# Low rows of features and gated values at a byte distance of their own from the weights

## The chip, the cores and the metric

The kernel runs on one NeuronCore of a Trainium2 chip. The metric is the device time of one execution in microseconds (us). Three executions of the kernel before took 1446.21, 1448.00 and 1448.74 us, median 1448.0.

## The reference

Two transformer blocks in float32 work on 256 context tokens and 256 latent tokens of width 1024. The first block mixes by a two-directional mLSTM and window attention, with a gated feed-forward network of width 2816. The second block has two layers, a retention and SSD mixer and multi-head latent attention, each with a SwiGLU network. Cut to the shape of the work that concerns us:

```python
def conv_glu(h, w_up, conv_w, conv_b, w_down):
    a, val = jnp.split(h @ w_up, 2, axis=-1)
    a = jax.nn.gelu(dwconv(a, conv_w, conv_b))
    return (a * val) @ w_down

def swiglu(h, w_gate, w_up, w_down):
    return (jax.nn.silu(h @ w_gate) * (h @ w_up)) @ w_down

x = x + g_a * (jnp.concatenate([y_m, y_a], axis=-1) @ w_out)
x = x + g_f * conv_glu(modulate(rmsnorm(x, norm_ffn), sh_f, sc_f), w_up, ffn_conv_w, ffn_conv_b, w_down)
...
u = modulate(rmsnorm(x, norm_mix), sh_a, sc_a) @ w_in
```

Nearly all of the arithmetic is such products of 1024 or 2816 features with weights.

## The kernel before

Activations stand transposed: 128 features on the partitions, 512 tokens (256 context, then 256 latent) along them. Every float32 operand of a linear product is split into a high part, rounded to the format that TensorE reads in one pass (fp32r), and a low part, the rest. A product is then three matmuls that add up in one PSUM bank: high weights with high features, high weights with low features, low weights with high features. I call such three matmuls over one tile of 128 features a k step. A unit of weights (128 outputs by 1024 features) has 8 k steps; `down` takes 22 tiles of gated values in parts of 8, 7 and 7.

The linear phases follow each other in a fixed order (`weight_phases`). Block 0 (latent tokens, 256 columns, except `ka` and `km`, which take all 512): `va_gates`, `ka`, `qa`, `vma`, `km`, `vmb`, `qm`, `om`, `out0`, `up0`, `down0`. Block 1 (512 columns): `in1`, `vra`, `vrb`, `out1`, `up1`, `down1`. Block 2: `ckv` (512), `cq`, `uk`, `uv`, `uq`, `out2`, `up2`, `down2` (256). In `out2`, `up2` and `down2` the high weights meet the high and the low features in one matmul instruction of two halves of 256 columns (`two_halves`, lines 621 to 624); the product that completes a tile of the output in `down2` is made of three. Other phases put high and low products of a unit in turn (`high_then_low`, lines 762 and 763) and then the 8 products of the low weights (768). In `va_gates`, `vma`, `vmb`, `vra` and `vrb` (`token_linear`) the roles are exchanged: features are loaded into the array and weights are streamed.

Weights go through three slots of 4096 bytes in each of `raw`, `w_hi` and `w_lo`. SyncE loads a unit into `raw` when GpSimd has split the unit that held the slot; ScalarE rounds it to `w_hi` (line 1502); GpSimd subtracts to get `w_lo` in two halves of 512 columns (line 2050); TensorE takes it. The order is written out, nothing is scheduled dynamically.

The features' high and low rows are two arrays of 8 x 512 floats in one room, `h_both`, the low array directly behind the high one (`rows_from`). The gated values are two arrays of 22 x 512 in `hidden_both` (`hidden`). Where the arrays start is set for each phase by constants: `MIXING` for the mixing phases of the three blocks, `UP_AT`, `DOWN_AT` and `OUT_AT` for the others. In a phase of 256 latent columns the latter three move the columns: they start at float 240 of each row in place of 256 (`columns`).

In bytes within a partition, the build places `w_hi` at 13440, `w_lo` at 25728, `hidden_both` at 87680 and `h_both` at 177792. A weight tile stands at a multiple of 512 from its slot, a feature row at a multiple of 2048. So the distance from the streamed row to the weights loaded for the next product, taken modulo 256, is one number for a phase. I call this the distance (loaded address minus streamed address, modulo 256).

Of the kernel before, what the change touches and what calls it, by code (L numbers as in the profile page):

```python
# [15 lines left out]
KD = D // P  # L16
CTX = LAT = 256
TOK = CTX + LAT
# [5 lines left out]
KF = FF // P  # L24
# [74 lines left out]

H_ROOM = 16
HIDDEN_ROOM = 0
MIXING = (16, 0, 16)
UP_AT = (240, 0, 240)
DOWN_AT = (240, 0, 240)
OUT_AT = (240, 0, 240)


CARRIED = {"ka": (1, 2), "qa": (2, 1), "vma": (1, 2), "km": (1, 3), "vmb": (1, 2), "qm": (1, 1), "om": (1, 1),  # L110
# [88 lines left out]
def build(nc, dram, small_at, tables_at, layers=3):  # L199
# [4 lines left out]
    with ExitStack() as stack:  # L204
# [3 lines left out]
        def sbr(name, shape):  # L208

            return stack.enter_context(nc.sbuf_tensor(name, shape, F32R))  # L210
# [31 lines left out]
        with nc.sbuf_tensor("arena", [P, ARENA], F32) as arena:  # L242
            pass
        with nc.sbuf_tensor("hidden_both", [P, HIDDEN_ROOM + 2 * KF * TOK], F32R) as hidden_room:
            pass

        def hidden(n):

            a = DOWN_AT[1] if n == 1 else 0
            both = hidden_room[:, a:a + 2 * KF * TOK].rearrange("p (a k t) -> p a k t", a=2, k=KF)  # L250
            return both, both[:, 0], both[:, 1]

        stack.enter_context(nc.sbuf_tensor("arena_end", [P, HIDDEN_ROOM + ARENA], F32))

        with nc.sbuf_tensor("scratch", [P, H_ROOM + 2 * KD * TOK], F32) as scratch_room:
            scratch = scratch_room[:, OUT_AT[1]:OUT_AT[1] + 2 * KD * TOK]
        h_room = sbr("h_both", [P, H_ROOM + 2 * KD * TOK])

        def rows_from(a):
            both = h_room[:, a:a + 2 * KD * TOK].rearrange("p (a k t) -> p a k t", a=2, k=KD)  # L260
            return both, both[:, 0], both[:, 1]

        def features(name):

            if name[:-1] in ("up", "out"):
                at = (UP_AT if name[:-1] == "up" else OUT_AT)[int(name[-1])]
                return rows_from(at if name in ("up1", "out1") else 0)
            return rows_from(MIXING[1 if name in ("in1", "vra", "vrb") else 2 if name in ("ckv", "cq") else 0])

        
        with nc.sbuf_tensor("work_r", [P, 3, TOK], F32R) as work_r:
            pass
        work = sb("work", [P, 3, TOK])
# [104 lines left out]
        ckv, rope_s, kpe, kswap = c(2, TOK), c(4, LAT), c(TOK), c(LAT)  # L378
# [96 lines left out]
        def columns(name, t0, t1):  # L475

            at = {"u": UP_AT, "d": DOWN_AT, "o": OUT_AT}[name[0]][int(name[-1])]
            return slice(at, at + LAT) if t0 == L0 else slice(t0, t1)
# [115 lines left out]
        def _(pe):  # L594
# [110 lines left out]
            def first_linear(gate):  # L705
                _, h_hi, h_lo = features("va_gates")

                f = ph["va_gates"]
                chunks = {0: (8, 9, 10, 11), 2: (12, 13, 14, 15)}
                for k in range(KD):  # L710
                    for q in chunks.get(k, ()):
                        ada_chunk(q)
                    if k == 2:
                        ada_columns(1)
                    u, n = divmod(k, KD // 2)
                    if n == 0:
                        pe.wait_ge(s["split"], 2 * (f.first_unit + u + 1))
                    w_h, w_l = (part_slot(x, f, u)[:, n * 144:n * 144 + 256] for x in (w_hi, w_lo))
                    gate(k)
                    for i in range(TT):  # L720
                        last = three(bank[i // 2][:, i % 2 * 256:i % 2 * 256 + 256], h_hi[:, k, i * P:(i + 1) * P],
                                     h_lo[:, k, i * P:(i + 1) * P], w_h, w_l, k == 0 and i % 2 == 0,
                                     k == KD - 1 and i % 2 == 1)
                        if k == KD - 1 and i % 2:
                            last.then_inc(s["steps"], 1)
# [21 lines left out]
            def linear(name, t0, t1, K=KD, both=None, hi=None, lo=None, M=P, gate=None, after=None, first=0, early=False):  # L747


                f = ph[name]  # L750
                both = features(name)[0] if both is None else both
                hi, lo = (both[:, 0], both[:, 1]) if hi is None else (hi, lo)
                n, parts = t1 - t0, f.parts
# [84 lines left out]
            def token_linear(name, K=KD, hi=None, lo=None, gate=None, after=None):  # L838

                f = ph[name]  # L840
                hi, lo = features(name)[1:] if hi is None else (hi, lo)
                pair = 2 if f.steps == 2 else 1
                for u in range(0, f.units, pair):
                    pe.wait_ge(s["split"], 2 * (f.first_unit + u + pair))
                    if pair == 2:
                        a, b = ((f.first_unit + u + i) % SLOTS for i in range(2))
                        two = slice(a, b + 1) if b > a else slice(a, None, -a)
                        w_h, w_l = ([x[:, two, 0:f.width].rearrange("p s (k n) -> p k s n", k=K)[:, k]
                                     for k in range(K)] for x in (w_hi, w_lo))
                    else:  # L850
                        w_h, w_l = ([part_slot(x, f, u, K)[:, k] for k in range(K)] for x in (w_hi, w_lo))
                    cols = pair * f.width // K
                    for i in range(TT):
                        t = f.first_taken + u * f.takes + i
                        room(t)
                        out = bank_of(t)[:, 0:cols]
                        if pair == 2:
                            out = out.rearrange("p (s n) -> p s n", s=2)
                        for k in range(K):
                            if gate and u == 0 and i == 0:  # L860
                                gate(k)
                            last = three(out, hi[:, k, i * P:(i + 1) * P], lo[:, k, i * P:(i + 1) * P],
                                         w_h[k], w_l[k], k == 0, k == K - 1)
                        last.then_inc(s["steps"], 1)
                    if after:
                        after(u)
# [534 lines left out]
            def ffn(n, t0, t1):  # L1401
                feature_sums(t0, t1, f"up{n}")
                linear(f"up{n}", t0, t1, gate=next_h(), early=True)
                linear(f"down{n}", t0, t1, K=KF, both=hidden(n)[0],
                       gate=lambda k: pe.wait_ge(s["hid_done"], KF * n + k + 1))
# [80 lines left out]
        def _(act):  # L1486
# [97 lines left out]
            def round_hidden(n, i, t0, t1):  # L1584

                act.wait_ge(s["hid_in"], KF * n + i + 1)
                act.activation(hidden(n)[1][:, i, columns(f"down{n}", t0, t1)], work[:, i % 3, t0:t1], ACT.Copy).then_inc(s["hid_round"], 1)  # L1587
# [548 lines left out]
        def _(dve):  # L2136
# [601 lines left out]
            def hidden_low(n, i, t0, t1):  # L2738

                dve.wait_ge(s["hid_round"], KF * n + i + 1)  # L2740
                own = columns(f"down{n}", t0, t1)
                low(hidden(n)[2][:, i, own], work[:, i % 3, t0:t1], hidden(n)[1][:, i, own]).then_inc(s["hid_done"], 1)
# [565 lines left out]
```

## Time and profile before

| | |
|---|---|
| Three executions, median | 1448.0 us |
| The profiled execution | 1450.16 us |
| its span, first to last instruction | 1448.4 us |
| mean granted clock of TensorE | 0.996 |
| TensorE, GpSimd, VectorE, ScalarE busy | 97%, 58%, 59%, 45% |

The span is about 1.8 us shorter than the execution's time. The durations of matmul rows are modelled ends of pipelined instructions: 389 ns for 512 columns is not what a product costs. The distance between two starts is. A row that merges several products gives the start of the first, and the next row's start closes the stretch. The counts of a stretch include up to three products that begin before it.

### The profile page before, as it was taken

What the parts mean: (1) busy time and instruction counts of PE and PEld (TensorE: products, weight loads), DVE (VectorE), ACT (ScalarE), POOL (GpSimd) and SP (SyncE); (2) the same over time, 40 slices, a digit from 0 to 9 for tenths busy, and PEclk for the clock granted to TensorE, in tenths of its full rate; (3) what the DMA queues carried; (4) which work ended last, traced back from release to release, by engine and by line L of the source; (5) the groups of instructions that cost most, each with busy time, mean ns of one, the idle gap of its engine ahead of it and who ended that gap; (6) DMA issues with size and microseconds to landing.
All of it is one profiled execution on the core that took longest, in us unless ns stands there. A gap on an engine that the chain in (4) does not pass through costs nothing.

```text
span 1448.4 us, 21620 instructions
## 1 busy us (share of the span) xinstructions
PE 1400.3 (97%) x8272; PEld 1167.9 (81%) x8272; DVE 847.7 (59%) x1638; ACT 657.7 (45%) x1069; POOL 839.2 (58%) x672
## 2 busy tenths in 40 slices
PE   5999999999999999889999999999999999999998
PEld 3977798999988889446788888888888966888887
DVE  3788667776668888687665333321136677644422
ACT  3555755455552234783332322322226386555442
POOL 1534426999855444785355544544446620799996
PEclk9999999999999999999999999999999999999999
DMA  9748415777767753001355555533333320456664
GB/s 366 289 166 302 173 42 201 252 259 232 260 227 248 238 178 106 18 30 59 131 198 189 195 195 188 196 108 97 103 95 115 118 81 8 140 182 188 188 193 127
DMA packets 71207, 242.01 MB, mean 167 GB/s; under 512 B 7488, under 2 KB 12992, under 8 KB 70720
## 3 DMA queue, kind: packets, MB, share of 16 engines
q1 hardware_dynamic: 68688, 236.63, 48.8%
q10 hardware_dynamic: 2416, 4.00, 0.9%
q8 instruction: 66, 1.08, 0.3%
q14 instruction: 37, 0.30, 0.1%
HBM read 238.50 MB, written 1.05 MB: 165 GB/s over the span
## 4 chain that ended last, share of the span: by engine, by line
PE 51%; DVE 4%; ACT 1%; issue 1%; POOL 0%; DMA 0%; DVEq 0%; ACTq 0%
PE bank L762 9%; PE bank L768 9%; PE bank L763 9%; PE bank L623 8%; PE bank L624 4%; PE bank L614 2%; PE bank L616 1%; PE bank L615 1%; DVE h_both L2282 1%; PE cond_a L1160 1%; PE bank L622 1%; PE bank L1160 1%; PE bank L1168 1%; PE cond_a L1221 1%; PE bank L1180 1%; PE cond_b L1180 1%
## 5 line engine op out<-in xcount | busy, mean ns | idle before, releaser
L2050 POOL TENSOR_TENSOR w_lo<-raw,w_hi 128x512 fp32r<-128x512 f32 (+2 forms) x610 | 775.7, 1301 | 577.5 <-ACT w_hi L1502 567.7
L1502 ACT ACTIVATE w_hi<-raw 128x1024 fp32r<-128x1024 f32 (+3 forms) x300 | 307.7, 1029 | 590.8 <-PE bank L768 345.9
L762 PE MATMUL bank<-h_both,w_hi 128*128 128x512 f32 (+1 forms) x1000 | 321.9, 340 | 0.4 <-ACT w_hi L1502 0.4
L763 PE MATMUL bank<-h_both,w_hi 128*128 128x512 f32 (+1 forms) x1000 | 321.2, 339 | 0.0
L762 PEld LDWEIGHTS bank<-h_both,w_hi 128*128 128x128 f32 x1000 | 188.1, 188 | 22.1 <-ACT w_hi L1502 0.6
L763 PEld LDWEIGHTS bank<-h_both,w_hi 128*128 128x128 f32 x1000 | 188.3, 188 | 21.3
L768 PE MATMUL bank<-h_both,w_lo 128*128 128x512 f32 (+1 forms) x1000 | 197.7, 340 | 0.3 <-POOL w_lo L2050 0.3
L768 PEld LDWEIGHTS bank<-h_both,w_lo 128*128 128x128 f32 x1000 | 159.8, 188 | 21.9 <-POOL w_lo L2050 0.7
L2164 DVE CUSTOM_DVE_ANT_0 ada_junk<-ada_w,cond_a 128x1024 bf16<-128x1024 f32 x128 | 153.8, 1216 | 13.5 <-DVE work L2733 8.1
L2146 DVE TENSOR_TENSOR hidden_both<-work,hidden_both 128x256 fp32r<-128x256 f32 (+1 forms) x66 | 56.1, 850 | 137.0 <-ACT hidden_both L1587 137.0
L623 PE MATMUL bank<-h_both,w_hi 128*128 128x512 f32 x345 | 124.4, 397 | 0.3 <-POOL w_lo L2050 0.2
L2720 DVE SCALAR_TENSOR_TENSOR X<-bank,mod,X 128x256 f32<-128x256 f32 x64 | 29.4, 481 | 146.8 <-PE bank L768 127.3
L762 PE MATMUL bank<-hidden_both,w_hi 128*128 128x256 f32 (+1 forms) x330 | 102.3, 331 | 0.0
L763 PE MATMUL bank<-hidden_both,w_hi 128*128 128x256 f32 (+1 forms) x330 | 102.3, 331 | 0.0
L624 PE MATMUL bank<-h_both,w_lo 128*128 128x256 f32 x345 | 97.0, 281 | 0.0
L2164 DVE CUSTOM_DVE_ANT_0 ada_junk<-ada_w,cond_b 128x1024 bf16<-128x1024 f32 x64 | 77.8, 1216 | 0.0
L623 PEld LDWEIGHTS bank<-h_both,w_hi 128*128 128x128 f32 x345 | 64.8, 188 | 14.7 <-POOL w_lo L2050 0.5
L614 PE MATMUL bank<-h_both,w_hi 128*128 128x256 f32 (+1 forms) x192 | 67.1, 349 | 3.6 <-DVE h_both L2282 1.6
L763 PEld LDWEIGHTS bank<-hidden_both,w_hi 128*128 128x128 f32 x330 | 62.2, 189 | 6.0
L762 PEld LDWEIGHTS bank<-hidden_both,w_hi 128*128 128x128 f32 x330 | 62.1, 188 | 6.0
L624 PEld LDWEIGHTS bank<-h_both,w_lo 128*128 128x128 f32 x345 | 64.7, 188 | 2.1
L615 PE MATMUL bank<-h_both,w_hi 128*128 128x256 f32 (+1 forms) x192 | 64.0, 333 | 0.0
(487 smaller groups left out, 2511.5 us busy)
## 6 DMA issues: line engine op xcount, KB each, us to landing
raw<-in_up SPq DMA_DIRECT2D x132, 512.0 KB, 3.6
ada_w<-in_ada SPq DMA_DIRECT2D x128, 512.0 KB, 4.5
raw<-in_down SPq DMA_DIRECT2D x48, 448.0 KB, 3.5
raw<-in_out SPq DMA_DIRECT2D x24, 512.0 KB, 3.5
raw<-in_down SPq DMA_DIRECT2D x24, 512.0 KB, 3.5
raw<-in_in SPq DMA_DIRECT2D x24, 512.0 KB, 5.3
arena<-in_ada SPq DMA_DIRECT2D x16, 512.0 KB, 11.7
raw<-in_uq SPq DMA_DIRECT2D x12, 384.0 KB, 3.0
```

Source lines behind the costliest of these rows:

```text
L614: pe.matmul(out, w_h, x_h, start=first, stop=False)
L615: pe.matmul(out, w_h, x_l, start=False, stop=False)
L623: pe.matmul(out.rearrange("p (h n) -> p h n", h=2), w_h, x_both, start=first, stop=False)
L624: return pe.matmul(out[:, 0:LAT], w_l, x_both[:, 0], start=False, stop=False)
L762: pe.matmul(out, w_h[:, k - k0], hi[:, k, cols], start=(k == 0), stop=False)
L763: pe.matmul(out, w_h[:, k - k0], lo[:, k, cols], start=False, stop=False)
L768: last = pe.matmul(out, w_l[:, k - k0], hi[:, k, cols], start=False, stop=(k == K - 1))
L1502: act.activation(part_slot(w_hi, f, u), raw_slot(f, u), ACT.Copy).then_inc(s["rounded"], 1)
L2050: pool.tensor_tensor(part_slot(w_lo, f, u)[:, a:b], raw_slot(f, u)[:, a:b], part_slot(w_hi, f, u)[:, a:b].bitcast(F32), ALU.subtract).then ...
L2146: return dve.tensor_tensor(out, x, hi.bitcast(F32), ALU.subtract)
L2164: dve.tensor_tensor_reduce(ada_junk[:, ada_sums[0] % 2, :], ada_w[:, k % SLOTS, :], silu_c[m][:, :], 1.0, 0.0, ALU.mult, ALU.add, mod[:, n ...
L2720: last = dve.scalar_tensor_tensor(out=X[:, k, a:e], in0=b[:, a - t0:e - t0], scalar=mod[:, layer[0] % 2, 8 * chunk + k, m:m + 1], in1=X[:, ...
```

## The change

The low rows no longer follow the high rows directly. Between them stand `LOW_AT` floats, another number for each phase. The rooms grow to hold this (`H_ROOM` from 16 to 112 floats, `HIDDEN_ROOM` from 0 to 64), which puts `h_both` 256 bytes higher (178048) and what follows it 640 bytes higher. In `down2` the latent columns start at float 224 in place of 240. Instructions, order, waits and shapes are the same on all engines.

```diff
-H_ROOM = 16
-HIDDEN_ROOM = 0
+H_ROOM = 112
+HIDDEN_ROOM = 64
 MIXING = (16, 0, 16)
 UP_AT = (240, 0, 240)
-DOWN_AT = (240, 0, 240)
+DOWN_AT = (240, 0, 224)
 OUT_AT = (240, 0, 240)
+LOW_AT = {'va_gates': 16, 'in1': 16, 'up1': 48, 'down1': 32, 'up0': 16, 'down0': 32, 'out0': 48, 'up2': 16, 'down2': 16, 'out2': 0, 'ckv': 32}
...
             a = DOWN_AT[1] if n == 1 else 0
-            both = hidden_room[:, a:a + 2 * KF * TOK].rearrange("p (a k t) -> p a k t", a=2, k=KF)
+            low = LOW_AT.get(f"down{n}", 0)
+            r = KF * TOK + low
+            both = hidden_room[:, a:a + 2 * r].rearrange("p (a r) -> p a r", a=2)[:, :, 0:KF * TOK]
+            both = both.rearrange("p a (k t) -> p a k t", k=KF)
...
-        def rows_from(a):
-            both = h_room[:, a:a + 2 * KD * TOK].rearrange("p (a k t) -> p a k t", a=2, k=KD)
+        def rows_from(a, low):
+            n = KD * TOK + low
+            both = h_room[:, a:a + 2 * n].rearrange("p (a r) -> p a r", a=2)[:, :, 0:KD * TOK]
+            both = both.rearrange("p a (k t) -> p a k t", k=KD)
...
         def features(name):
 
+            low = LOW_AT.get(name, 0)
             if name[:-1] in ("up", "out"):
                 at = (UP_AT if name[:-1] == "up" else OUT_AT)[int(name[-1])]
-                return rows_from(at if name in ("up1", "out1") else 0)
-            return rows_from(MIXING[1 if name in ("in1", "vra", "vrb") else 2 if name in ("ckv", "cq") else 0])
+                return rows_from(at if name in ("up1", "out1") else 0, low)
+            n = 1 if name in ("in1", "vra", "vrb") else 2 if name in ("ckv", "cq") else 0
+            return rows_from(MIXING[n], LOW_AT.get(("va_gates", "in1", "ckv")[n], 0))
```

The distances that come out of this, modulo 256 bytes:

| phases | columns | k steps | before, high and low | after, high | after, low |
|---|---|---|---|---|---|
| `qa`, `qm`, `om` | 256 | 96 | 192 | 192 | 128 |
| `ka`, `km` | 512 | 40 | 192 | 192 | 128 |
| `out0` | 256 | 64 | 64 | 64 | 128 |
| `up0` | 256 | 352 | 64 | 64 | 0 |
| `down0` | 256 | 176 | 64 | 64 | 192 |
| `in1` | 512 | 192 | 0 | 0 | 192 |
| `out1` | 512 | 64 | 0 | 0 | 0 |
| `up1` | 512 | 352 | 0 | 0 | 64 |
| `down1` | 512 | 176 | 0 | 0 | 128 |
| `ckv`, `cq` | 512, 256 | 24, 48 | 192 | 192 | 64 |
| `out2` | 2 x 256 | 64 | 64 | 64 | 64 |
| `up2` | 2 x 256 | 352 | 64 | 64 | 0 |
| `down2` | 2 x 256 | 176 | 64 | 128 | 64 |
| `vma`, `vmb` (features loaded) | 256 | 64 | 64 | 64 | 128 |
| `vrb` (features loaded) | 256 | 32 | 0 | 0 | 64 |

`uk`, `uv` and `uq` read other arrays, which do not move; in `uk` the distance is 256 bytes and so 0 modulo 256.

## Rows read from the trace of the kernel before

**Rows 1.** The page's busy shares and granted clock by slice.

```profile
span 1448.4 us, 21620 instructions
PE 1400.3 (97%) x8272; PEld 1167.9 (81%) x8272; DVE 847.7 (59%) x1638; ACT 657.7 (45%) x1069; POOL 839.2 (58%) x672
PEclk9999999999999999999999999999999999999999
```

**Rows 2.** The page's chain of waits, shares of the span.

```profile
PE 51%; DVE 4%; ACT 1%; issue 1%; POOL 0%; DMA 0%; DVEq 0%; ACTq 0%
```

**Rows 3.** GpSimd's groups in `up0`, then `up2`: busy us, mean ns, idle us.

```profile
L2050 POOL TENSOR_TENSOR w_lo<-raw,w_hi 128x512 fp32r<-128x512 f32 x73 | 94.5, 1331 | 5.6 <-ACT w_hi L1502 5.2
L2050 POOL TENSOR_TENSOR w_lo<-raw,w_hi 128x512 fp32r<-128x512 f32 x65 | 87.9, 1389 | 3.4 <-ACT w_hi L1502 3.4
```

**Rows 4.** Timeline, TensorE, `up1`: start us, duration us, instruction.

```profile
900.08 0.39 PE L762 MATMUL bank<-h_both,w_hi 128*128 128x512 f32 x1
...
900.76 0.39 PE L763 MATMUL bank<-h_both,w_hi 128*128 128x512 f32 x1
```

**Rows 5.** Stretches, TensorE, in `up0`, `down0`, `down1`, `up2`.

```profile
255.00:353.60 98.60, 98.60 (x840) 1.00 0.73 250
353.60:415.80 62.20, 62.20 (x531) 1.00 0.75 239
953.60:1073.10 119.50, 119.50 (x529) 1.00 0.33 98
1287.00:1377.10 90.10, 90.10 (x513) 1.00 0.62 188
```

**Rows 6.** Timeline, TensorE, early in `up0`.

```profile
238.04 0.28 PE L762 MATMUL bank<-h_both,w_hi 128*128 128x256 f32 x1
...
238.61 0.28 PE L763 MATMUL bank<-h_both,w_hi 128*128 128x256 f32 x1
```

**Rows 7.** Timeline, TensorE, later in `up0`.

```profile
301.77 1.11 PE L768 MATMUL bank<-h_both,w_lo 128*128 128x256 f32 x8
302.71 0.28 PE L762 MATMUL bank<-h_both,w_hi 128*128 128x256 f32 x1
```

**Rows 8.** Timeline, TensorE, `up2`.

```profile
1301.79 0.40 PE L623 MATMUL bank<-h_both,w_hi 128*128 128x512 f32 x1
...
1302.14 0.40 PE L623 MATMUL bank<-h_both,w_hi 128*128 128x512 f32 x1
```

**Rows 9.** Timeline, TensorE, `vrb`.

```profile
574.10 0.28 PE L616 MATMUL bank<-w_hi,h_both 128*128 128x256 f32 x1
574.22 0.28 PE L614 MATMUL bank<-w_hi,h_both 128*128 128x256 f32 x1
```

**Rows 10.** Timeline, TensorE, `km`.

```profile
92.01 0.39 PE L614 MATMUL bank<-h_both,w_hi 128*128 128x512 f32 x1
...
92.70 0.39 PE L614 MATMUL bank<-h_both,w_hi 128*128 128x512 f32 x1
```

**Rows 11.** Timeline, TensorE, `up1` after a wait.

```profile
724.58 0.40 PE L615 MATMUL bank<-h_both,w_hi 128*128 128x512 f32 x1
...
725.53 0.39 PE L616 MATMUL bank<-h_both,w_lo 128*128 128x512 f32 x1
725.75 0.39 PE L614 MATMUL bank<-h_both,w_hi 128*128 128x512 f32 x1
```

**Rows 12.** Timeline, TensorE, `uk`.

```profile
1117.93 0.39 PE L615 MATMUL bank<-ckv_lo,w_hi 128*128 128x512 f32 x1
1118.16 0.39 PE L616 MATMUL bank<-ckv_hi,w_lo 128*128 128x512 f32 x1
```

**Rows 13.** Stretches, TensorE, in `qa` and `cq`, two stretches.

```profile
52.40:68.20 15.80, 15.80 (x136) 1.00 0.95 356
1097.00:1112.50 15.50, 15.50 (x136) 1.00 0.54 167
```

## The prediction

> **What bounds the kernel now.** I read the page's shares first. [...] The chain that ended last is 51% TensorE in matmuls of the linear phases, with 4% and less for any other engine; the rest is too finely cut to be listed [rows 2]. So only what TensorE pays per product, or a stall that starves it, moves the time. The other engines matter in one place: GpSimd, which makes `w_lo`, has 5.6 us of idle time in 98.6 us of `up0` and 3.4 in 90.1 us of `up2` [rows 3].
>
> The next question is what one product costs. The duration of a matmul row is modelled, so I use start to start. With all 512 columns streamed (second block) products start every 226.7 ns: 900.08 to 900.76 is three of them [rows 4]; `down1` holds this for all its 528 products (119.5 us / 528 = 226.3) [rows 5]. With 256 columns there are two paces at the very same addresses. Early in `up0` products start every 113.3 ns (238.04 to 238.61 is five of them, 0.57 us) [rows 6]. Later, 301.77 to 302.71 is eight of them, 117.5 to 118 each [rows 7], and this slower pace holds from about 251 us through `up0` and all of `down0`: 62.2 us / 528 = 117.8 ns [rows 5]. In the third block a two-half product and its low product together take 0.35 us, 1301.79 to 1302.14 being one of the pairs [rows 8], the same 353.3 ns as three products at 117.8. In `vrb` every product takes 120 ns [rows 9]. In `km` (512 columns, distance 192) three products take 92.01 to 92.70, 0.69 us against 0.68 at distance 0 [rows 10]. After an interruption the 512-column phase does not return to 226.7 at once: 724.58 to 725.53 is four products, 0.95 us, before it settles [rows 11].
>
> I read this as follows. 113.3, 120, 226.7, three at 353.3 and three in `km` at about 687 are 17, 18, 34, 53 and 103 times 6.67 ns. [...]
>
> **What can be won at all.** The best steady pace that any row shows is 113.3 ns for 256 columns and 226.7 for 512. Against it the second block (`in1`, `out1`, `up1`, `down1`) has nothing to give. The 256-column phases can give up to 353.3 - 340 = 13.3 ns for each k step (three products).
>
> **The change part by part.** The instructions, their order, their waits and their shapes are the same on every engine; only addresses move. Nothing is added for VectorE, ScalarE, GpSimd or the DMA queues; I price their moved addresses at nothing, and a kernel-wide loss there would have to go through TensorE's feeding, which has slack except in `up2` (below).
>
> 1. All of `h_both`, `work` and `spare` move up by 256 bytes or more. `uk` reads its features at a distance of 256 bytes and settles at 0.23 us per product like distance 0 [rows 12], so a move by 256 is worth nothing.
>
> 2. The low rows of `up0`, `down0`, `out0`, `qa`, `qm`, `om`, `cq` (256 columns) go from the common distance to another one. Bounds: if these k steps all reach 51 slots they give back 13.3 ns each; if the moved product locks at 18 slots as in `vrb`, while the two others stay, they lose 2.2 ns each (120 - 117.8). [...] `up0` from 255 us: 840/24 = 35 units of 8 k steps [rows 5] = 280 x 6.67 = 1.9 us. `down0`: 176 x 6.67 = 1.2 us. The smaller ones show 15.8 and 15.5 us for 136 counted products [rows 13], 116 and 114 ns, and with three at the edge taken off 119 and 117; about 32 + 32 + 22 (`om`) + 60 + 32 = 178 k steps, 1.2 us. `ka` and `km` have 40 k steps with 6.7 ns to lose or win: 0.1 us, left out. The same goes for `va_gates`, `vma`, `vmb`, `vra`, where features are the loaded side (124 k steps, up to 0.8 us either way), and for `vrb`, whose low loads move from 0 to 64: 0 to 0.6 us, left out.
>
> 3. `up2`: high and low rows are one instruction here, and the load of the next weights falls in its first half. [...] One slot again would bring a unit from 2.81 us (90.1 x 16 / 513) [rows 5] to 2.76. But GpSimd needs 2 x 1.389 = 2.78 us for the unit's low weights [rows 3], so it becomes the bound: 0.03 x 44 = 1.4 us at most. For `up0` the same sum gives 2 x 1.331 = 2.66 us against 2.82 - 0.05, which leaves the gain whole [rows 3].
>
> 4. `down2`: the high distance goes from 64 to 128 and the low one stays at 64, since the columns start 16 earlier. 154 of its 176 k steps are at 53 slots (the last tile, three products each, is not): 1.0 us by the same rule, between +2.1 and -1.3 us (8.3 ns per step, the difference of 235 to 226.7 in [rows 8, 4]). `out2` is unchanged.
>
> 5. The second block: high distance 0 stays, the low one becomes 192 (`in1`), 64 (`up1`), 128 (`down1`). `out1` keeps 0. No row shows such a pair. [...] Ceiling: 8.3 ns for each low product. [...]
>
> Sum: 1.9 + 1.2 + 1.2 + 1.4 + 1.0 = 6.7 us. The profiled execution took 1450.2 us (span 1448.4 [rows 1]) and gives 1443.5; the runs' median is 1448.0, 2.2 below it, which gives 1441.3.
>
> [...]
>
> **Rivals.**
> A. *Own distance, slower.* Each product pays for the distance between its own stream and the next load, and nothing locks anew. Then the change spoils the second block, the only part that is free of loss: `up1`'s 352 low products go from 226.7 to the 233 to 235 of distance 64 [rows 8]: 352 x 6.7 = 2.4 us; `in1`'s 192 pay 2.3 ns as in `km`: 0.4 us; `down1`'s 176 pay up to 8.3: 1.5 us; `up0`'s 352 go to the 120 of `vrb`: 0.8 us. Together 5.1 us, 1453.1. For it: each pace above belongs to a distance. Against it: `up0` has two paces at one distance. It decides once a low product of the second block costs over 3 ns.
> B. *Nothing.* The lock depends on when a phase starts after a wait, not on the low rows: 1448.0. For it: the two paces of `up0`. Against: `vrb` and `down1` never leave theirs.
> C. *A pace below 226.7 in the second block.* [...] One start distance of the settling products is 0.22 us (725.53 to 725.75), below 226.7 [rows 11]. Saving 6.67 ns on the 720 low products of `in1`, `up1`, `down1` is 4.8 us more: 1436.5. Against it: that one follows slower ones and may only make up for them; the lowest steady pace is 226.7.
> D. *Everything at 51 slots.* 280, 176 and 178 k steps at 13.3 ns are 8.4 us, with `down2` 2.1 and `up2` still held by GpSimd at 1.4: 11.9 us, 1436.1.
>
> **How the numbers follow.** Chances: forecast 0.38, D 0.12, C 0.08, A 0.24, B 0.18. A measurement of this kernel tells 0.2% (2.9 us) from no change. Forecast, C and D are faster by more, 0.58; B is within, 0.18; A is slower, 0.24. The range runs from all ceilings of gain together less a little (D with half of C, 1433) to A with a small surplus, 1454. The forecast's own range is 1437 to 1445.
>
> **What would show it.** Right: in `up0` and `down0` the starts of three products 346.7 ns apart, `down0` at 61.0 us or less for its 528; in `up2` GpSimd without idle time and ScalarE's rounding ending what TensorE waits for; `down1` unchanged at 119.5 us. Wrong: `up1` longer than 240.7 us (A), `down0` at 62.2 again (B), starts nearer than 226 ns in the second block (C), 340 ns per k step (D). An `up0` that changes pace midway would say that the wait before it and not the distance sets the lock.

## The result, and the profile after

The changed kernel takes 1454.62 us (median of four runs, 1450.51 to 1455.84) against 1448.37 us before (1446.21 to 1449.25). The ratio is 1.0033, with a 95% interval of 1.0017 to 1.0048: slower, by about 4.8 us. The prediction said 1441.3, and its range ended at 1454. The profiled execution took 1455.84 us, its span 1454.0.

First the page of the changed kernel, the lines that answer to [rows 1, 2].

```profile
span 1454.0 us, 21620 instructions
PE 1406.5 (97%) x8272; PEld 1169.2 (80%) x8272; DVE 852.8 (59%) x1638; ACT 657.7 (45%) x1069; POOL 839.7 (58%) x672
PE 50%; DVE 5%; ACT 2%; issue 1%; POOL 1%; DMA 0%; DVEq 0%; ACTq 0%
```

TensorE has the same 8272 matmuls and 6.2 us more of busy time. No other engine took its place: VectorE, the next one, has 5% of the chain that ended last, against 4% [rows 2]. So the loss is in what a product costs, and the stretches of the phases show where. These are stretches of TensorE in the changed kernel, each from the phase's first start to its last: `up0`, `down0`, `in1`, `up1`, `down1`, `up2`, `down2` (length, busy, count, clock, DMA share, GB/s).

```profile
225.66:351.77 126.11, 124.90 (x1055) 1.00 0.67 231
351.88:413.68 61.80, 61.80 (x530) 1.00 0.76 241
419.87:554.64 134.77, 134.30 (x580) 1.00 0.61 204
714.40:957.13 242.73, 242.20 (x1056) 1.00 0.53 184
957.36:1078.16 120.80, 120.80 (x529) 1.00 0.32 97
1258.84:1382.65 123.81, 123.10 (x716) 1.00 0.58 177
1382.88:1444.65 61.77, 61.77 (x375) 1.00 0.58 166
```

The same stretches of the kernel before:

```profile
226.91:353.48 126.57, 125.62 (x1056) 1.00 0.67 230
353.60:415.66 62.06, 62.06 (x529) 1.00 0.75 240
421.85:554.06 132.21, 131.57 (x579) 1.00 0.62 207
712.81:953.35 240.54, 239.91 (x1055) 1.00 0.53 185
953.58:1073.03 119.45, 119.45 (x528) 1.00 0.33 98
1252.01:1376.99 124.98, 124.63 (x716) 1.00 0.58 175
1377.22:1438.97 61.75, 61.75 (x375) 1.00 0.57 166
```

Read line by line, `in1` is 2.6 us longer, `up1` 2.2 and `down1` 1.3: 6.1 us in block 1. `up0` gives back 0.5, `down0` 0.3 and `up2` 1.2; `down2` nothing. That is 4.2 us net of the span's 5.6. The changed execution also has three stretches between the feed-forward phases, 3.4 us each, in which the granted clock is 0.50 (from 583.5, 665.4 and 1177.4 us), where the one before has two (from 637.0 and 650.7 us). By my estimate one costs about 1.7 us, half its length. Their number is not tied to the change: `e3_rooms_only` (below), with the distances of before, has one, and `best_block2`, whose profiled execution took 1445.41 us, has three.

Now the starts in block 1, the answer to [rows 4]. In `down1` of the changed kernel (distance 0 for line 769, the products with high rows, and 128 for line 770, those with low rows):

```profile
1002.85 0.39 PE L769 MATMUL bank<-hidden_both,w_hi 128*128 128x512 f32 x1
1003.08 0.40 PE L770 MATMUL bank<-hidden_both,w_hi 128*128 128x512 f32 x1
1003.31 0.39 PE L769 MATMUL bank<-hidden_both,w_hi 128*128 128x512 f32 x1
1003.54 0.40 PE L770 MATMUL bank<-hidden_both,w_hi 128*128 128x512 f32 x1
1003.77 0.39 PE L769 MATMUL bank<-hidden_both,w_hi 128*128 128x512 f32 x1
...
1004.23 0.39 PE L769 MATMUL bank<-hidden_both,w_hi 128*128 128x512 f32 x1
```

Two products take 0.46 us, three such pairs 1.38 us from 1002.85 to 1004.23, where before they took 1.36. From all starts of the phase a high product takes 226.4 ns, a low one 233.8, one of the low weights 226.7. The moved product pays 7 ns, one step, and the others keep their pace. In `in1` (low distance 192) the gaps within a unit of 24 products vary from 225 to 241 ns. Here are the first and the last of six starts, and the same two starts one unit later:

```profile
500.43 0.40 PE L770 MATMUL bank<-h_both,w_hi 128*128 128x512 f32 x1
...
501.60 0.40 PE L769 MATMUL bank<-h_both,w_hi 128*128 128x512 f32 x1
...
505.99 0.40 PE L770 MATMUL bank<-h_both,w_hi 128*128 128x512 f32 x1
...
507.16 0.40 PE L769 MATMUL bank<-h_both,w_hi 128*128 128x512 f32 x1
```

Five products take 1.17 us both times, 234 ns each here and 231.7 over the phase. Those whose own distance is still 0 pay more than the moved ones (232.1 against 230.8). The cost repeats all the same, but over a unit and not over a product: four in five stretches of 24 products in the phase take 5560 ns, 834 steps of 6.67 ns, against 5440 ns, 816 steps, before. In `up1` (low distance 64) the unit takes 5493 ns, 824 steps. Its eight products of low weights:

```profile
801.70 2.01 PE L775 MATMUL bank<-h_both,w_lo 128*128 128x512 f32 x8
803.54 0.40 PE L769 MATMUL bank<-h_both,w_hi 128*128 128x512 f32 x1
```

They take 1.84 us, and 230.7 ns each over the phase. The first seven products behind them take 229.9 ns each; the last nine are back at 226.5, the pace of before, as low ones of 225 and high ones of 228 in turn. In the kernel before `up1` settled in a similar way after a wait, four products in 0.95 us [rows 11]; whether the two are the same was not shown.

In `up2` the answer to [rows 8] is, three starts of line 630 apart by one k step each:

```profile
1332.84 0.39 PE L630 MATMUL bank<-h_both,w_hi 128*128 128x512 f32 x1
...
1333.18 0.39 PE L630 MATMUL bank<-h_both,w_hi 128*128 128x512 f32 x1
...
1333.53 0.40 PE L630 MATMUL bank<-h_both,w_hi 128*128 128x512 f32 x1
```

Two k steps take 0.69 us, 346.7 ns each to the nearest step, where [rows 8] have 353.3: the one step of 6.67 ns that was forecast. Not every k step gives it. Of 296 such pairs 249 take 52 steps, but 39, about one in each unit, take 54; a unit of 8 k steps takes 417 steps in place of 423, so it gives six steps and not eight.

### The profile page after: what moved, and what is told of

Same layout as the page of the kernel before. It is cut to its first block, busy times and chain, and to the rows that moved or that the text cites. A ratio compares the mean times of both kernels' runs of the same rounds, so it can differ in the third digit from the quotient of the medians.

```text
span 1454.0 us, 21620 instructions
## 1 busy us (share of the span) xinstructions
PE 1406.5 (97%) x8272; PEld 1169.2 (80%) x8272; DVE 852.8 (59%) x1638; ACT 657.7 (45%) x1069; POOL 839.7 (58%) x672
## 4 chain that ended last, share of the span: by engine, by line
PE 50%; DVE 5%; ACT 2%; issue 1%; POOL 1%; DMA 0%; DVEq 0%; ACTq 0%
PE bank L770 9%; PE bank L775 9%; PE bank L769 9%; PE bank L630 7%; PE bank L631 4%; PE bank L621 1%; PE bank L623 1%; PE bank L622 1%; PE cond_a L1167 1%; DVE h_both L2289 1%; PE bank L629 1%; PE bank L1167 1%; PE bank L1175 1%; PE cond_b L1187 1%; PE bank L1187 1%
## 5 line engine op out<-in xcount | busy, mean ns | idle before, releaser
L2153 DVE TENSOR_TENSOR hidden_both<-work,hidden_both 128x256 fp32r<-128x256 f32 (+1 forms) x66 | 61.4, 930 | 136.1 <-ACT hidden_both L1594 136.1
L621 PE MATMUL bank<-h_both,w_hi 128*128 128x256 f32 (+1 forms) x192 | 67.7, 353 | 3.3 <-DVE h_both L2289 1.3
L623 PE MATMUL bank<-h_both,w_lo 128*128 128x256 f32 (+1 forms) x192 | 64.8, 337 | 0.0
```

The source lines that it names most:

```text
L621: pe.matmul(out, w_h, x_h, start=first, stop=False)
L623: return pe.matmul(out, w_l, x_h, start=False, stop=last)
L2153: return dve.tensor_tensor(out, x, hi.bitcast(F32), ALU.subtract)
```

## The experiments

Three questions stood after this. Is it the distances of block 1 that cost the time? Is it the distance modulo 256 bytes, or the position of the arrays as such? And does a product pay for its own distance, or for the pair?

**`e1_block1_zero`: block 1 set back.**

```diff
-LOW_AT = {'va_gates': 16, 'in1': 16, 'up1': 48, 'down1': 32, ...
+LOW_AT = {'va_gates': 16, 'in1': 0, 'up1': 0, 'down1': 0, ...
```

> The change with the low distances of in1, up1 and down1 set back to that of their high rows, all else as changed. Theory A (each product pays for the distance between its own stream and the next load, and a 512-column lock is lost): these three phases return to 226.7 ns per product, 6.1 us less than the changed kernel (in1 2.6, up1 2.2, down1 1.3), and about 1448 us or 1 to 2 us below the kernel before, since up0 and up2 keep their gain. Rival N (the loss came from half-clock stretches and waits that differ by chance): the time stays at 1452 to 1455 us.

Measured: 1447.93 us, ratio to before 0.999 (0.998 to 1.000). Its `in1`, `up1`, `down1` and `up2`:

```profile
420.96:553.13 132.17, 131.54 (x579) 1.00 0.62 209
710.25:950.76 240.51, 239.89 (x1056) 1.00 0.53 185
950.99:1070.44 119.45, 119.45 (x529) 1.00 0.32 98
1249.49:1372.80 123.31, 123.09 (x715) 1.00 0.58 178
```

Block 1 is back at its length of before within 0.04 us in each phase, while `up2` keeps its gain. The three entries hold the whole loss. Rival N (the expectation's name for chance) falls.

**`e2_block1_only`: those entries alone.**

```diff
+LOW_AT = {'in1': 16, 'up1': 48, 'down1': 32}
```

(with `down2`'s columns at 240 again)

> Only the low distances of in1, up1 and down1 are changed (192, 64, 128), all others as before. Theory A: about 6 us slower than before, 1454 us; in down1 the products with low rows take 233 to 234 ns, the others 226.7; in in1 no steady pace. Rival N: within 0.2% of before.

Measured: 1455.75 us, ratio 1.0039 (1.0024 to 1.0054), 5.7 us slower. Its `in1`, `up1`, `down1`:

```profile
420.85:555.62 134.77, 134.29 (x579) 1.00 0.60 205
714.20:956.91 242.71, 242.21 (x1055) 1.00 0.53 184
957.14:1077.94 120.80, 120.80 (x528) 1.00 0.32 97
```

These are the lengths of the changed kernel to 0.02 us. The loss is not a matter of chance or of what else the change does in the other phases.

**`e3_rooms_only`: the arrays moved, the distances not.** `LOW_AT = {}` and `down2` at 240, with the rooms of the change.

> All low distances zero and the columns of down2 at 240, but the rooms as in the change, so that everything behind the arena stands 256 to 640 bytes higher. Theory A with a period of 256 bytes: each phase has its pace of before within 0.3 ns, the time is that of before within 0.2%. Rival P (the position of the arrays counts beyond 256 bytes, or for the other engines): some phase or the whole is off by more, up to the 6 us that the change costs.

Measured: 1449.29 us, ratio 0.9995 (0.9985 to 1.0005). `up1` is 240.50 us and `down1` 119.45 us long, as before. `up0` is 125.02 against 126.57, a point taken up below.

**`m64`: all low rows of `h_both` a full 256 bytes further.** (`LOW_AT` 64 for each of its phases, `down2`'s columns at 240, the gated values as before.)

> The low rows of h_both stand 64 floats (256 bytes) further away in every phase, hidden_both as before. If the distance counts modulo 256: every phase has its pace of before (up1 226.8, in1 226.9, up0 117.1, km 229.3 ns) and the time is 1446 to 1450 us. If the longer distance itself matters, in1 and up1 are at 229 ns and more, and the time is 4 us and more above before.

Measured: 1445.89 us in its one run; `in1` 226.84, `up1` 226.74, `up2` in 124.97 us. Every pace with a fixed value is that of before. The distance counts modulo 256 bytes, and step 1 of the prediction holds.

**`m16`, `m32`, `m48`: one value for every phase.** `LOW_AT` is 16, 32 or 48 floats in every phase, with `down2`'s columns at 240. All phases of block 1 then have the same pair of distances, which shows whether a pace belongs to the pair or to the phase.

> All phases with the low rows 16 floats (64 bytes) further from the high ones: low distance is the high one less 64. Theory A: in1 as in the change, 231 ns; up1 and down1 (0 and 192) and out1 lose their 226.7, to 228 to 232; up0 and up2 keep what they have in the change (116.3 ns, and 229 + 117 per pair); down0 (64 and 0) drops to near 116.3 as up0 did, since both have the same pair of distances. Rival: the pace belongs to the phase and its waits, and down0 stays at 117.3 to 117.8.

> All phases with the low rows 32 floats (128 bytes) further. Theory A: in1, up1 and out1 behave as down1 does in the change (low product 233 to 234, others 226.7, mean 229.1), with one third of the products paying 7 ns; up0 (64 and 192) behaves as down0 in the change, 117.3. Rival: the pace belongs to the phase; in1 and up1 are then not at 229.1.

> All phases with the low rows 48 floats (192 bytes) further. Theory A: in1, down1 and out1 behave as up1 does in the change (products with high and low rows in turn at 226.7 in the mean, the run of low weights at about 231, mean 229); up0 and down0 (64 and 128) as out0 in the change, 118.2. Rival: the pace belongs to the phase, and in1 is elsewhere.

Measured: 1459.82, 1453.18 and 1460.32 us (one run each; before on the same chip 1448.02). Mean start to start per product, in ns, from the starts within a phase, with gaps above 260 ns (waits) left out:

| distances of block 1, high and low | `in1` | `out1` | `up1` | `down1` | kernels |
|---|---|---|---|---|---|
| 0, 0 | 226.9 | 227.7 | 226.8 | 226.7 | before |
| 0, 128 | 229.1 | 230.5 | 229.1 | 228.9 | `m32` |
| 0, 192 | 231.6 | 231.6 | 231.7 | 231.2 | `m16` |
| 0, 64 | 229.1 | 229.2 | 229.0 | 230.2 | `m48b`, for `down1` `m48` |

The pace belongs to the pair: with one pair four phases agree within 1.6 ns. (`in1` of the changed kernel, with 0 and 192, has 231.7.) The pair 0 and 128 gives the plain rule, one product in three one step longer (`m32`: in `up1` 226.1 ns for high products, 234.0 for low ones, 226.6 for those of the low weights). `m32`'s starts in `up1` show it, low products in lines 770:

```profile
799.63 0.39 PE L769 MATMUL bank<-h_both,w_hi 128*128 128x512 f32 x1
799.86 0.40 PE L770 MATMUL bank<-h_both,w_hi 128*128 128x512 f32 x1
800.10 0.39 PE L769 MATMUL bank<-h_both,w_hi 128*128 128x512 f32 x1
800.32 0.40 PE L770 MATMUL bank<-h_both,w_hi 128*128 128x512 f32 x1
800.55 0.39 PE L769 MATMUL bank<-h_both,w_hi 128*128 128x512 f32 x1
```

`down0` in `m16` came to 116.65 ns, near the 116.3 that was expected. `m48` failed as a test for `h_both`: its room for gated values had to be larger, which moved `h_both` by 384 bytes, so that its high rows stood at other distances too. It is of use for `down0`, `down1` and `down2` alone. The next run repeats it with the right base.

**`m48b`: 48 floats, base kept.**

> Low rows of h_both 48 floats (192 bytes) further in every phase, h_both's base as before modulo 256 (in m48 it was 384 bytes off, so that its high rows had moved by 128 too), hidden_both as before. Theory A: up1 as in the change, 229.0; in1 and out1, which now have the same pair (0 and 64), also 228.5 to 229.5; up2 near 170.9; time near 1453 us. Rival (the pace belongs to the phase): in1 elsewhere, such as the 231.3 it has with low distance 192.

Measured: 1452.14 us; `in1`, `up1`:

```profile
420.82:554.13 133.31, 132.78 (x579) 1.00 0.61 207
711.36:954.09 242.73, 242.21 (x1056) 1.00 0.52 183
```

`up1` has the length of the changed kernel again, and `in1`, with `up1`'s pair in place of its own, drops from 134.77 to 133.31 us. The rival that a pace belongs to the phase falls. In `up2` the expectation missed by 1 ns: 171.9 ns per product against 170.9, with units of 417, 418 and 419 steps.

**`b1_common`: block 1 at other distances, but equal ones.** (With `LOW_AT = {}`.)

```diff
-MIXING = (16, 0, 16)
-UP_AT = (240, 0, 240)
-DOWN_AT = (240, 0, 240)
+MIXING = (16, 16, 16)
+UP_AT = (240, 48, 240)
+DOWN_AT = (240, 32, 240)
```

> Low distances equal to the high ones everywhere, but the common distance of block 1 moved from 0 to 192 (in1), 64 (up1) and 128 (down1). Theory A in its strict form (each product pays for its own distance, whatever its neighbours): in1 229.3 as km, up1 about 228.0 (what the products at distance 64 took in the changed kernel), down1 233.3 for all its products, so down1 3.5 us longer. Rival U (a pair of unequal distances costs, one common distance does not): in1, up1 and down1 below the 231.3, 229.0 and 229.2 of the changed kernel. The lock form (a distance has its own repeating cycle that a mixed pair breaks): in1 and up1 on short repeating cycles, not on wandering ones.

Measured: 1461.46 us, one run. `in1`, `up1`, `down1`:

```profile
421.46:554.77 133.31, 132.73 (x579) 1.00 0.60 206
713.91:961.11 247.20, 246.79 (x1056) 1.00 0.51 180
961.34:1084.31 122.97, 122.97 (x529) 1.00 0.31 95
```

and the first and the last of six starts in its `up1`:

```profile
800.11 0.40 PE L770 MATMUL bank<-h_both,w_hi 128*128 128x512 f32 x1
...
801.27 0.39 PE L769 MATMUL bank<-h_both,w_hi 128*128 128x512 f32 x1
```

Five products take 1.16 us. With one common distance the mean over a phase is 228.9 ns at 192, 233.3 at 64 and 233.3 at 128: 34 1/3, 35 and 35 steps of 6.67 ns, against 34 at distance 0. `down1` grew by 3.5 us as expected, and `in1` came to 228.9 against the 229.3 expected. Its units take 824 steps, those of `up1` 840, on cycles of three products (226, 229 and 232 ns) and of two (231 and 236 ns) that repeat, as the lock form said. Rival U falls for 64 and 128, where equal distances cost more than the mixed pairs (233.3 against 229.0); for 192 it holds, 228.9 against 231.7. And the strict form misjudged `up1`: it took 228.0 from mixed pairs and got 233.3. So a product's own distance does not set its cost alone; what else does was not shown. Distance 0 is the only one of the four measured at which a 512-column phase rests on 34 steps.

One rival stands against all of this. These runs move the streamed rows of block 1 and never its weights, so the streamed address alone, modulo 256, could set the cost. `vrb` bears on it, where the weights are streamed from fixed addresses and the features are loaded. Its 96 products before (distances 0 and 0), in the changed kernel (0 and 64) and in `b1_common` (64 and 64):

```profile
568.74:580.22 11.48, 11.48 (x99) 1.00 0.40 135
569.32:580.60 11.28, 11.28 (x99) 1.00 0.43 135
569.45:580.32 10.87, 10.87 (x99) 1.00 0.41 143
```

That is 119.9, 117.8 and 113.4 ns per product with waits left out. The first two come back in other kernels: 119.9 in `e3_rooms_only` and `m64` (0 and 0), 117.8 in `e2_block1_only` and `m16` (0 and 64). So the loaded address counts too, and 113.4 is, within 0.1 ns, the faster of the two paces that `up0` has at 64 and 64. A cost that follows the distance fits both, but no run moved both operands together.

**`best_block2` and `best_blocks02`: the part that gains.** (Rooms as in the change, `down2`'s columns at 240.)

```diff
+LOW_AT = {'up2': 16, 'down2': 16, 'out2': 16}
...
+LOW_AT = {'up2': 16, 'down2': 16, 'out2': 16, 'up0': 16, 'down0': 16}
```

> Low rows 16 floats further in up2, down2 and out2 alone, all other distances as before. Theory A: block 0 and 1 as before; up2 1.4 to 1.6 us, down2 0.7, out2 0.2 us shorter: 2.4 us below before, ratio 0.9983. Rival N: no difference, ratio 1.000 within its interval.

> As the one with block 2 alone, and up0 and down0 too have their low rows 16 floats further. Theory A: up0 at 116.3 and down0 at 116.65 ns in every run, against 114.0 to 117.1 and 114.6 to 117.8 by chance without; 2 to 4 us below before, ratio 0.997 to 0.9985, and within 1 us of the one with block 2 alone. Rival N: ratio 1.000.

Measured, against before on the same chip at 1449.46 us: 1447.93 us, ratio 0.999 (0.9977 to 1.0003), for block 2 alone, and 1447.76 us, ratio 0.9983 (0.9972 to 0.9994), with blocks 0 and 2. The second's `up0`, `down0`, `up2`, `down2`:

```profile
227.57:354.54 126.97, 124.48 (x1056) 1.00 0.66 233
354.65:416.13 61.48, 61.48 (x530) 1.00 0.73 238
1252.16:1375.45 123.29, 123.16 (x715) 1.00 0.58 180
1375.68:1436.66 60.98, 60.98 (x375) 1.00 0.55 165
```

`up2` is 1.7 us shorter than before, `down2` 0.8 and `down0` 0.6. This version is faster than the kernel before by 0.17%, which its interval just tells from nothing, and by less than the 2 to 4 us expected. Block 2 alone, expected at 0.9983, is not told from 1, though in its profile `up2` is 2.0 us and `down2` 0.8 us shorter. `up0` is not shorter at all; in `best_blocks02` TensorE is idle in it for 2.5 us, against 0.9 before. Its length with both distances at 64 was 126.57, 126.78, 125.02, 124.74, 126.68 and 125.25 us (before, `e2_block1_only`, `e3_rooms_only`, `m64`, `b1_common`, `best_block2`), mean 125.8; with 64 and 0 it was 126.11, 125.15, 125.58 and 126.97 (after, `e1_block1_zero`, `m16`, this one), mean 126.0. These lengths include waits. Without them the pair 64 and 0 has 116.3 ns per product in all four kernels (units of 418 steps), while equal distances have 113.5 to 117.1: two paces, 113.3 (408 steps) and 117.8 (424 steps), both of which occur within `up0` of one execution. The mixed pair sits between the two. `down0` is the same: 60.87 to 62.07 us at equal distances, 61.47 and 61.48 with 64 and 0.

## Why the prediction was wrong, step by step

- *What bounds the kernel, and the step of 6.67 ns*, which the prediction also calls a slot: right. In the twelve further executions most units of 24 products in `in1` and `up1` take one number of such steps in any one phase, 816, 824, 834, 837 or 840, and of the phases' difference of 4.2 us 3.9 are busy time of TensorE. In `in1` with 0 and 192 a unit (834 steps), and not a product or a k step, is what repeats.
- *Step 1, a move by 256 bytes is nothing*: right (`e3_rooms_only`, `m64`).
- *Step 5, the second block*: this is the step that failed. Its sum has nothing for three moved phases, and no row stood for such a pair. They lost 6.1 us. The ceiling was written beside it, 8.3 ns for each low product, which for 720 of them is 6.0 us. (The 235 ns in it is not in [rows 8]; the trace of before has 233.8 for that product.) The prediction itself had said that this block has nothing to give; it did not draw from it that a move could then only cost, at every distance since measured. In `down1` the high products hold 226.4 ns, but that does not spare the moved one, which alone pays (7 ns x 176 = 1.2 us of 1.35). In `in1` they do not: they take 232.1 ns, more than the 230.8 of the moved ones.
- *Step 2, one step for each 256-column k step*: mis-sized. 1.9 us were expected of `up0`, 1.2 of `down0` and 1.2 of the small phases. The changed kernel shows 0.5 and 0.3, and the small phases nothing: `qa` and `cq` went from 117.8 to 117.2 ns per product at best, `out0` from 117.7 to 118.4. `vma` and `vmb`, left out as either way, went from 115.9 and 115.1 to 118.2 and 118.3. Where `up0` ran at 424 steps per unit the pair gives 6 steps and not the 8 forecast, but it also takes 10 from the units that ran at 408. No run shows the 6.67 ns for each k step that the sum has here: with 64 and 0 the pace repeats over a unit, at 418 steps. `down0`'s 0.6 us with low distance 0 is within what equal distances do by themselves.
- *Step 3, `up2`*: right in kind, and nearly right in size, 1.2 us against 1.4, in part by luck. The 1.4 was a cap set by GpSimd on a gain of eight steps per unit; the gain is six steps, 1.8 us for 44 units, less some 0.6 us of waits and settling early in the phase. The cap did not bind: GpSimd's group in most of the changed `up2`, which answers to [rows 3], has 1.382 us for a half, 2.76 us for a unit, where TensorE needs 2.77, and TensorE waited for it once, 0.6 us.

```profile
L2057 POOL TENSOR_TENSOR w_lo<-raw,w_hi 128x512 fp32r<-128x512 f32 x65 | 87.4, 1382 | 2.4 <-ACT w_hi L1509 2.4
```

  Which low distance it is hardly matters: `m16`, `m32`, `m48b` and the change have low distances 0, 192, 128 and 0 and all come to 123.5 to 123.9 us. In all four the jump between the two halves is not a multiple of 256 bytes, which is the same as that the two distances differ.
- *Step 4, `down2`*: 1.0 us expected, none found. With the high rows left at 64, as in `m16`, it gives 0.8. The moved columns (distance 128) took it back.
- *Rival A* had the right place. Its sum, +5.1 against +4.8, is luck: it has 4.3 us for the three phases that lost 6.1, and nothing of the 2.0 us that `up0`, `down0` and `up2` gave back. Its terms: `up1` 2.4 against 2.2, `down1` 1.5 against 1.35, `in1` 0.4 against 2.6, `up0` +0.8 against -0.5. Its 120 ns for the pair with 0 in `up0` came out as 116.3, and `vrb` itself left 120. *Rival B*, in which a phase's start after a wait sets the pace that it keeps (its lock), fell with the interval. *C*: no steady pace below 226.7 was found in any kernel; the low products of `up1` at 225 are followed by high ones at 228. *D* fell, though `down0` and `up0` reached 113.5 in the run of `best_block2`, at equal distances. `e2_block1_only` changes addresses alone and costs 5.7 us; the streamed address counts in block 1 (226.7 against 228.9 to 233.3 ns) and the loaded one in `vrb` (119.9, 117.8 and 113.4 ns). By what way they count was not shown.

What stays open: why 64 and 192 with 0 behave as they do. The paces were read from starts alone, which do not show what a product waits for, and no experiment moved weights and features by the same amount, which would tell the distance from the two addresses.

## What to carry to other kernels

Before an address is moved, ask of each phase whether its pace has anything to give. For a phase that runs at the best pace seen, as block 1 did with 226.7 ns, expect a loss: every other distance tried there cost time (228.9 to 233.3 ns in the mean). Where a stream and the load of the next weights run side by side, treat their distance (here modulo 256 bytes: `m64` has the paces of before) as a setting of the phase, read starts and not durations, sum them over the group of products that repeats, and test one value in all phases at once: one profile then prices each phase, and the choices can be put together.

## What the runs showed of the hardware that was not expected

- `up1` at distances 0 and 64 repeats to 0.02 us in kernels that differ elsewhere: 242.73 us in the changed kernel, 242.71 in `e2_block1_only`, 242.73 in `m48b`. `up0` at 64 and 64 (256 columns) does not: 126.57 us in the kernel before, 124.74 in `m64`. It has two paces there, 4% apart: 113.3 and 117.8 ns, in most units of `m64` the first, in most of the kernel before the second. The distance does not say which.
- A 512-column product of this format took at least 34 steps of 6.67 ns, 226.7 ns, in the mean of every steady stretch of these kernels; matmuls of 512 columns on float32 operands that are not rounded (line 1160 of the kernel before, 96 rows) start every 429 ns. With unequal distances the single gaps of the products wander between 224 and 241 ns (`in1` of the changed kernel and of `m16`), and yet 24 of them sum to the same whole number of steps in most units (834 in `in1`, 824 in `up1` of the changed kernel).
- In `up2`, where the moving operand of a matmul is in two halves, a unit takes 417 steps in most cases (the changed kernel, `m16`, `m32`, `best_block2`), or 418 and 419 (`m48b`), in place of 423 (before, `m64`), when the low half does not start a multiple of 256 bytes after the high one.
